# A joining stage whose first token tile is split: heads ahead of the line, weight rows taken in another order, gate rows loaded by another stage

## The chip, the cores and the metric

One NeuronCore of a Trainium2 chip runs the whole program in one launch. The metric is device microseconds (us) of that core, the median of several executions; lower is better. Engines: PE (TensorE, matrix products), DVE (VectorE), ACT (ScalarE), POOL (GpSimd), SP (SyncE, which here only issues DMAs and waits). Each engine runs its own instructions strictly in the written order, and the engines meet through semaphores.

## The reference, cut to what matters

The program is a two-layer transformer trunk (1024 image tokens and 256 context tokens, width 1024). The change is in the end of the first layer's mixer. Each token has a convolution branch of 512 channels and four attention heads of 128 channels; they are normed, joined and multiplied by one 1024 x 1024 weight:

```
def conv_module(a):
    u = a[..., :A_WIDTH] * jax.nn.sigmoid(a[..., A_WIDTH:])
    u = depthwise_conv(u, conv_w, conv_b)
    return jax.nn.silu(layer_norm(u, ln_g, ln_b))

def merge(ya, ob):
    yb = (rms_norm(ob, subln_g) * (1 - lambda_init)).transpose(0, 2, 1, 3).reshape(bsz, t, B_WIDTH)
    return jnp.concatenate([ya, yb], axis=-1) @ w_out
...
x = x + mx[2] * rms_norm(yx, norm_mix_post[i])
hx = modulate(rms_norm(x, norm_ffn_pre[i]), mx[3], mx[4])
```

## The kernel before, in words

The program is a chain of stages, each a block with one hand-written instruction list for each engine. A stage ends in a barrier that all five engines reach; then the semaphores are cleared, and a second barrier starts the next stage. The change is in the joining stage (`join_project`, signals and tiles named `out0_` or `out_`) and in the last lines of the stage ahead of it, the differential attention (`da_`), whose SP list already issues the joining stage's loads through the object `joined` (`JoinInputs`).

The joining stage works on ten tiles of 128 tokens, t = 0 to 9 (N = 10). A tile lies in `uo` as 8 blocks of 128 channels by 128 tokens: blocks 0 to 3 (AT = 4) are "the line" (the convolution branch, layer norm over its 512 channels), blocks 4 to 7 are the four heads (one rms norm each). For one tile:

- `mean(t)` on PE sums the line over channels with a matrix of ones; `centre(t)` on DVE takes the mean off the line.
- `square_heads(t)` and `square_line(t)` on ACT square both; `sums(t)` on PE adds the squares up over channels with one-column products (four for the heads, four for the line).
- `mean_squares(t)` on DVE, `inverse_roots(t)` on POOL (a power of -1/2 of 128x5 numbers) and `spread(t)` on PE (five transposes that put the factors along the tokens) give the norm factors; `normalise(t)` on DVE multiplies the line (L3299), then the heads (L3300).
- `finish(t)` on ACT takes four Silu of the line and rounds the whole tile to `y_hi`; `split(t)` on DVE takes the rest `y_lo`, and signals `y_ready`.
- The product on PE, `step(t, k, half)`, is three passes of 512 columns (hi*hi, hi*lo, lo*hi; L88 to L90) for each of 8 weight rows k and 2 halves of the output: 48 matmuls a tile.
- After it (`copy`, `residual`, `square_x`, `norm`, `turn`, `modulated`, `rest`) come the post norm with the gate rows, the residual with the old x, and the pre norm of the next stage.

LEAD = 2: while PE multiplies tile t, it also does `mean`, `sums` and `spread` of tile t + 2 between the products.

The weight rows have to be split too: `weights(k)` on ACT rounds row k of `work` to `w_hi` (signal `w_hi_done`), `weights(k)` on DVE takes the rest `w_lo` (signal `w_ready`). The eight raw rows lie in `work[:, 0..7]`, and the slots are used again: X = 2 means that the old x of tiles 0, 1, 2 goes to slots 2, 3, 4, so SP's `load_x(t)` waits until the row in that slot is split. Behind these loads SP's list has `inputs(2)`, the load of tile 2's tokens, which waits for `y_ready` of tile 0, because tile 2 takes tile 0's buffer; then the post gain into slot 7.

PE's list starts `mean(0)`, `sums(0)`, `mean(1)`, `spread(0)`, `sums(1)`, and then tile 0's product, which waits for `y_ready` of the whole tile and takes the rows in the order 0 to 7, with `spread(1)`, `mean(2)` and `sums(2)` between them; `spread(2)` follows the product. On ACT, `square_heads(t + 2)` stands ahead of `finish(t + 1)`; on DVE, `centre(t + 2)` stands ahead of `split(t + 1)`.

Of the kernel before, what the change touches and what calls it, by code (L numbers as in the profile page):

```python
# [15 lines left out]
P = 128  # L16
# [2541 lines left out]
def diff_attention(nc, head, joined, o_heads, qk, v_rows, ident, silu, mod, ada_w, ada_b, ada_first):  # L2558
# [60 lines left out]
    with ExitStack() as ctx:  # L2619
# [30 lines left out]
        def _(sp):  # L2650
# [321 lines left out]
def join_project(nc, joined, y_hi, y_lo, post_gain, x_old, x_new, ident, first, more_hi, more_lo, even_ps, sums_ps, first_acc,  # L2972
# [10 lines left out]
    POST, PRE = 0, 3  # L2983

# [3 lines left out]
    with ExitStack() as ctx:  # L2988
        def sb(label, shape, dt=F32):
# [11 lines left out]
        minus_half = sb("minus_half", [P, NORMS])  # L3001

# [10 lines left out]
            "x_done", "pre_squared", "pre_ms", "pre_rstd", "h_done", "h_turned", "f_done", "h_hi", "h_lo", "last_f", "last_hi"], inherited=joined.handles))  # L3013
# [14 lines left out]
        def _(sp):  # L3028
# [20 lines left out]
            for t in range(3):  # L3049
# [18 lines left out]
        def _(pe):  # L3068
# [12 lines left out]
            def sums(t):  # L3081
# [3 lines left out]
                if t == 1:  # L3085
                    pe.wait_ge(s.normed.sem, 1)
# [6 lines left out]
            def spread(t):  # L3093
# [3 lines left out]
                if t == 0:  # L3097
                    pe.wait_ge(s.centred.sem, 2)
                elif t == 1:
# [6 lines left out]
            def step(t, k, half):  # L3106
                cols_ = slice(half * BANK, (half + 1) * BANK)
                return exact_product(pe, ps[t % 2][:, cols_], y_hi[:, k, tokens(t)], y_lo[:, k, tokens(t)],
                                     w_hi.at(k)[:, cols_], w_lo.at(k)[:, cols_], k == 0, k == KD - 1)
# [13 lines left out]
            sums(0)  # L3123
            mean(1)
            spread(0)
            sums(1)
            for t in range(N + 2):
                if t >= 2:
# [19 lines left out]
                if t == 0:  # L3148
                    for k in range(KD):
                        pe.wait_ge(s.w_ready.sem, k + 1)  # L3150
                        for half in range(2):
                            mm = step(t, k, half)
                        if k == 0:
                            spread(1)
                        if k == 4:
                            mean(LEAD)
                        if k == 6:
                            sums(LEAD)
                    mm.then_inc(s.y_full.sem, 1)
                    spread(LEAD)  # L3160
                    continue
                for k in range(KD):
                    step(t, k, 0)
                    if k == 3:
                        mean(t + LEAD)
                for k in range(KD):
# [4 lines left out]
                spread(t + LEAD)  # L3171
# [1895 lines left out]
```

## Time and profile before

| | |
|---|---|
| median of 3 runs | 3247.48 us (3243.46 to 3247.98) |
| the profiled execution | 3244.99 us, of which the span of the profile is 3242.2 us |
| mean granted TensorE clock | 0.981 of full speed |
| PE busy | 3114.3 us, 96% of the span |
| DVE, ACT, POOL busy | 2196.7, 1358.1, 581.1 us |
| joining stage | from 615.7 us of the span to about 790 us |

Times below are us from the start of the span. "Idle before" an instruction is the time in which its engine did nothing ahead of it, with what ended that. A granted clock of 1.00 is the upper of TensorE's two levels (2.4 GHz), 0.50 the lower one (1.2 GHz).

### The profile page before, as it was taken

To read this page: it belongs to the slowest core of one execution; us is meant where nothing else is said; L and a number is where in the kernel's file an instruction comes from. 1 tells how busy PE (TensorE), PEld (TensorE's weight loads), DVE (VectorE), ACT (ScalarE), POOL (GpSimd) and SP (SyncE) were. 2 spreads that over 40 slices of the span, in tenths; PEclk is the share of its full clock that TensorE was granted. 3 is DMA by queue.
4 is the path that set the end of the run, shared out by engine and by line. 5 is a ranking of instruction groups with operands and counts; after the bars stand their busy time and mean duration, and the time that the engine had idled before them with its cause. 6 is when DMAs were issued, how large, how long until landed. Compare 5 with 4: busy or idle time off the path is not lost. (4 is left out here: it accounts for less than half of the span.)

```text
span 3242.2 us, 42850 instructions
## 1 busy us (share of the span) xinstructions
PE 3114.3 (96%) x16442; PEld 2557.2 (79%) x16442; DVE 2196.7 (68%) x2463; ACT 1358.1 (42%) x2275; POOL 581.1 (18%) x603
## 2 busy tenths in 40 slices
PE   7999899899999999999998999999999999999997
PEld 5888777788999999988797776666667788888875
DVE  4999767556756656679644346777774676776777
ACT  5222455466323323444565313444443433333444
POOL 0001000121222222233022100000001123332323
PEclk8999999899999999999999999999999999999998
DMA  7224786523122122566734743233312222222765
GB/s 219 69 93 133 220 264 219 195 98 90 57 73 79 56 78 69 181 212 201 240 129 148 260 145 70 46 84 71 73 36 78 85 83 80 85 78 89 241 205 196
DMA packets 302527, 415.70 MB, mean 128 GB/s; under 512 B 108878, under 2 KB 206862, under 8 KB 301302
## 3 DMA queue, kind: packets, MB, share of 16 engines
q1 hardware_dynamic: 288950, 363.29, 36.5%
q0 software_dynamic: 13376, 49.69, 4.1%
q8 instruction: 131, 2.15, 0.3%
q14 instruction: 70, 0.57, 0.1%
HBM read 318.65 MB, written 94.13 MB: 127 GB/s over the span
## 5 line engine op out<-in xcount | busy, mean ns | idle before, releaser
L2160 DVE TENSOR_TENSOR ring_lo<-raw_rows,ring_hi 128x512 fp32r<-128x512 f32 x200 | 181.8, 910 | 203.1 <-ACT ring_hi L2011 202.8
L4672 ACT ACTIVATE mla_e<-mla_scores 128x512 f32<-128x512 f32 x320 | 190.2, 598 | 307.9 <-PE mla_scores L90 297.0
L1283 PE MATMUL banks<-y_hi,ring_hi 128*128 128x384 f32 (+2 forms) x688 | 221.2, 322 | 4.5 <-DVEq L2148 3.9
L1285 PE MATMUL banks<-y_hi,ring_lo 128*128 128x384 f32 (+2 forms) x688 | 221.3, 322 | 0.0
L1284 PE MATMUL banks<-y_lo,ring_hi 128*128 128x384 f32 (+2 forms) x688 | 221.1, 321 | 0.0
L1283 PE MATMUL banks<-differences,ring_hi 128*128 128x512 f32 (+2 forms) x560 | 192.6, 344 | 3.4 <-ACT sums L2021 2.6
L1284 PE MATMUL banks<-differences,ring_hi 128*128 128x512 f32 (+2 forms) x560 | 192.3, 343 | 0.0
L1285 PE MATMUL banks<-differences,ring_lo 128*128 128x512 f32 (+2 forms) x560 | 192.2, 343 | 0.0
L862 DVE SCALAR_TENSOR_TENSOR ab_work<-ab_work,ab_taps 128x1295 f32<-128x1295 f32 x120 | 188.0, 1567 | 3.3
L4710 DVE TENSOR_REDUCE mla_least<-mla_rounded 128x1 f32<-128x1024 f32 x128 | 154.9, 1220 | 36.7 <-PE mla_rounded L4584 36.7
L2011 ACT ACTIVATE ring_hi<-raw_rows 128x512 fp32r<-128x512 f32 x200 | 125.2, 626 | 114.0 <-PE accs L1285 57.3
L1283 PE MATMUL accs<-y_hi,ring_hi 128*128 128x512 f32 (+1 forms) x464 | 165.9, 358 | 3.9 <-DVE ring_lo L3648 2.6
L1285 PE MATMUL accs<-y_hi,ring_lo 128*128 128x512 f32 (+1 forms) x464 | 165.6, 357 | 0.0
L1284 PE MATMUL accs<-y_lo,ring_hi 128*128 128x512 f32 (+1 forms) x464 | 165.5, 357 | 0.0
L2093 ACT ACTIVATE ring_hi<-raw_rows 128x512 fp32r<-128x512 f32 x154 | 97.1, 631 | 158.9 <-DMA raw_rows<-in_ffn_w_down 43.5
L4728 DVE TENSOR_TENSOR mla_acc<-mla_acc,mla_e 128x1024 f32<-128x1024 f32 x128 | 156.4, 1222 | 10.7 <-ACT mla_e L4672 5.1
L4616 PE MATMUL mla_out<-mla_e,ckv 128*64 128x512 f32 x640 | 155.0, 605 | 0.0
L2303 DVE TENSOR_TENSOR ring_lo<-raw_rows,ring_hi 128x512 fp32r<-128x512 f32 x154 | 125.3, 814 | 38.5 <-ACT ring_hi L2093 37.2
L1283 PEld LDWEIGHTS banks<-y_hi,ring_hi 128*128 128x128 f32 x688 | 129.7, 188 | 9.4 <-DVEq L2148 4.2
L1285 PEld LDWEIGHTS banks<-y_hi,ring_lo 128*128 128x128 f32 x688 | 129.8, 189 | 4.4
L1284 PEld LDWEIGHTS banks<-y_lo,ring_hi 128*128 128x128 f32 x688 | 129.8, 189 | 4.4
L88 PE MATMUL ab_main<-h_hi,da_first_k_hi 128*128 128x512 f32 (+1 forms) x360 | 131.4, 365 | 0.5 <-DVE da_first_k_lo L842 0.5
(561 smaller groups left out, 8711.2 us busy)
## 6 DMA issues: line engine op xcount, KB each, us to landing
raw_rows<-in_ffn_w_up SPq DMA_DIRECT2D x88, 512.0 KB, 3.6
da_ada_w<-in_ada_w SPq DMA_DIRECT2D x10, 4096.0 KB, 14.5
raw_rows<-in_ffn_w_down SPq DMA_DIRECT2D x110, 256.0 KB, 3.1
raw_rows<-in_ffn_w_down SPq DMA_DIRECT2D x44, 512.0 KB, 4.3
out_raw<-scratch_act SPq DMA_DIRECT2D x66, 256.0 KB, 3.4
sums<-scratch_act SPq DMA_DIRECT2D x55, 256.0 KB, 3.5
ab_raw<-in_ab_w_in SPq DMA_DIRECT2D x20, 512.0 KB, 3.9
scratch_act<-conv_lines SPq DMA_DIRECT2D x20, 512.0 KB, 4.8
```

The costliest lines, as they stand in the source:

```text
L88: pe.matmul(out, a_hi, b_hi, start=first, stop=False)
L862: dve.scalar_tensor_tensor(out=out, in0=src[:, j:j + SPAN], scalar=taps[:, i, j:j + 1], in1=out, op0=ALU.mult, op1=ALU.add)\
L1283: pe.matmul(out, w_hi[:, w], b_hi[:, a:a + n], start=start and k == 0, stop=False, skip_group_check=True)
L1284: pe.matmul(out, w_hi[:, w], b_lo[:, a:a + n], start=False, stop=False, skip_group_check=True)
L1285: mm = pe.matmul(out, w_lo[:, w], b_hi[:, a:a + n], start=False, stop=k == KD // 2 - 1, skip_group_check=True)
L2011: act.activation(blocks(begun.hi(r)), source(r), ACT.Copy).then_inc(s.w_hi, weight(r))
L2160: dve.tensor_tensor(blocks(begun.lo(r)), source(r), blocks(begun.hi(r)).bitcast(F32), ALU.subtract)\
L2303: dve.tensor_tensor(begun.lo(r), down_source(j, i), begun.hi(r).bitcast(F32), ALU.subtract).then_inc(s.down_lo, 1)
L4616: mm = pe.matmul(o_ps[c * C_V:(c + 1) * C_V, :], v[:, h % 2, kt, :], e[:, (h * KT + kt) % E_SLOTS, c * BANK:(c + 1) * BANK], start=kt == 0 ...
L4672: act.activation(e[:, tile % E_SLOTS, c * BANK:(c + 1) * BANK], s_ps[:, score_fill(h, i) % 3, :], ACT.Exp)\
L4710: dve.tensor_reduce(least[:, 0, t:t + 1], src, AX.X, ALU.max, negate=True).then_inc(s.piece_least.sem, 1)
L4728: dve.tensor_tensor(out, before, e[:, tile % E_SLOTS, :], ALU.add).then_inc(s.added.sem, 1)
```

## The change

Six column and gate loads (`load_rows`) leave the end of the attention stage's SP list and stand in the joining stage's SP list, behind its four stores and ahead of the x loads; their wait for stored modulation rows goes. Tile 0 is worked in two halves of channels. The heads have sums, mean square, inverse root, spread, norm, rounding and rest of their own, with signals of their own (`heads_...`), ahead of the line. The weight rows are rounded and split in the order `FIRST_ORDER` = 4, 5, 6, 7, 0, 1, 2, 3, and tile 0's product takes them in that order: four head rows once `heads_ready` is there, then four line rows once `y_ready` is there. What stood between PE's products is placed anew in tiles 0, 1 and 2. ACT touches a Silu of one column ahead of the first real one. The core of the diff:

```diff
             joined.load_tokens(sp, 0)
             joined.load_tokens(sp, 1)
-            sp.wait_ge(s.row0_stored.sem, 64)
-            sp.wait_ge(s.row1_stored.sem, 32)
-            joined.load_rows(sp)
...
                 if t < 3:
-                    sp.wait_ge(s.w_ready.sem, X + t + 1)
+                    sp.wait_ge(s.w_ready.sem, FIRST_ORDER.index(X + t) + 1)
...
             joined.store_tails(sp)
-            for t in range(3):
+            joined.load_rows(sp)
+            for t in (2, 0, 1):
                 load_x(t)
             sp.wait_ge(loaded.tail_stored.sem, 32)
             inputs(2)
...
+            def first_heads():
+                pe.wait_ge(s.squared.sem, 1)
+                for j in range(B_HEADS):
+                    mm = pe.matmul(head_ps[:, j:j + 1], sq[:, AT + j, :], ones[:, 0:1], start=True, stop=True)
+                mm.then_inc(s.heads_full.sem, 1)
...
+            def spread_first_line():
+                pe.wait_ge(s.rstd_done.sem, 1)
+                pe.wait_ge(s.centred.sem, 2)
+                pe.transpose(line_ps, rstd[:, 0, B_HEADS:NORMS].broadcast_to([P, P]), ident[:, :]).then_inc(s.spread.sem, 1)
...
             mean(0)
-            sums(0)
+            first_heads()
+            first_line()
+            spread_first_heads()
             mean(1)
-            spread(0)
-            sums(1)
...
+                if t == 0:
+                    pe.wait_ge(s.heads_ready.sem, 1)
+                    for n, k in enumerate(FIRST_ORDER):
+                        if k == 0:
+                            pe.wait_ge(s.y_ready.sem, 1)
+                        pe.wait_ge(s.w_ready.sem, n + 1)
+                        for half in range(2):
+                            mm = step(t, k, half, FIRST_ORDER)
+                        if k == AT:
+                            spread_first_line()
+                        if k == KD - 1:
+                            sums(1)
+                        if k == 1:
+                            spread(1)
+                    mm.then_inc(s.y_full.sem, 1)
+                    mean(2)
+                    continue
                 pe.wait_ge(s.y_ready.sem, t + 1)
...
                     step(t, k, 0)
+                    if t == 1 and k == 2:
+                        sums(2)
+                    if t == 1 and k == 6:
+                        spread(2)
...
                     mm = step(t, k, 1)
+                    if t == 1 and k == 1:
+                        mean(3)
-                    if k == 2:
+                    if k == (4 if t == 1 else 2):
                         sums(t + LEAD)
...
             act.wait_ge(loaded.small_in.sem, 48)
             square_heads(0)
-            weights(0)
-            weights(1)
+            for k in FIRST_ORDER[0:2]:
+                weights(k)
             square_line(0)
-            for k in range(2, 6):
+            for k in FIRST_ORDER[2:4]:
                 weights(k)
+            act.activation(table[:, :], gains[:, 0:1], ACT.Silu).then_inc(s.table.sem, 1)
+            round_first_heads()
+            weights(FIRST_ORDER[4])
             square_heads(1)
+            weights(FIRST_ORDER[5])
             square_line(1)
-            finish(0)
-            weights(6)
-            weights(7)
+            finish_first_line()
+            for k in FIRST_ORDER[6:]:
+                weights(k)
...
             mean_squares(1)
-            weights(6)
-            weights(7)
+            for n in range(6, KD):
+                weights(n)
             for t in range(N + 3):
                 normalise(t + 1)
+                if t == 1:
+                    residual(0)
                 centre(t + LEAD)
```

How the lists stand now is shown at three places. SP, at the end of the attention stage and the start of the joining stage (the two branches are the stage's end and the next one's start); before:

```order
L2927 DMA out_uo<-scratch_o_heads 128x4x128
L2944 DMA out_cols<-scratch_mod 128x8x1
L2946 DMA out_cols<-scratch_mod 128x8x1
L2944 DMA out_cols<-scratch_mod 128x8x1
L2946 DMA out_cols<-scratch_mod 128x8x1
L2949 DMA out_gates<-scratch_mod 128x1024 x2
L2619 UNCONDITIONAL_BRANCH
L3027 UNCONDITIONAL_BRANCH
L2918 DMA scratch_o_heads<-out_heads_out 128x256 x2
L2921 DMA scratch_mod<-out_mod_rows 4x256 x2
L3042 DMA out_work<-in_x 128x1024 x3
```

and now:

```order
L2924 DMA out_uo<-scratch_o_heads 128x4x128
L2619 UNCONDITIONAL_BRANCH
L3027 UNCONDITIONAL_BRANCH
L2915 DMA scratch_o_heads<-out_heads_out 128x256 x2
L2918 DMA scratch_mod<-out_mod_rows 4x256 x2
L2941 DMA out_cols<-scratch_mod 128x8x1
L2943 DMA out_cols<-scratch_mod 128x8x1
L2941 DMA out_cols<-scratch_mod 128x8x1
L2943 DMA out_cols<-scratch_mod 128x8x1
L2946 DMA out_gates<-scratch_mod 128x1024 x2
L3042 DMA out_work<-in_x 128x1024 x3
L2924 DMA out_uo<-scratch_conv 128x4x128
```

The six loads stand behind the branch to the next stage, and the three x loads still stand ahead of tile 2's tokens. PE, from the first mean of the joining stage to the first products (`out_sums` and `out_heads` are the banks of the sums, `accs` the output bank of tile 0, `ring` and `upper` the tiles that hold weight rows 4 to 7); before:

```order
L3078 MATMUL out_sums<-out_uo,out_ones 128x128 x4
L3088 MATMUL out_sums<-out_ones,out_sq 128x1 x4
L3090 MATMUL out_sums<-out_ones,out_sq 128x1 x4
L3078 MATMUL out_sums<-out_uo,out_ones 128x128 x4
L3101 MATMUL out_sums<-ident,out_rstd 128x128
L3103 MATMUL out_heads<-ident,out_rstd 128x128 x4
L3088 MATMUL out_sums<-out_ones,out_sq 128x1 x4
L3090 MATMUL out_sums<-out_ones,out_sq 128x1 x4
L88 MATMUL accs<-out_w_hi,y_hi 128x512
```

and now:

```order
L3079 MATMUL out_sums<-out_uo,out_ones 128x128 x4
L3108 MATMUL out_heads<-out_ones,out_sq 128x1 x4
L3114 MATMUL out_sums<-out_ones,out_sq 128x1 x4
L3120 MATMUL out_heads<-ident,out_rstd 128x128 x4
L3079 MATMUL out_sums<-out_uo,out_ones 128x128 x4
L88 MATMUL accs<-ring_hi,y_hi 128x512
```

`sums(1)` (L3088 and L3090 for the second time) is no longer ahead of the products; it follows the 24 matmuls of the head rows. DVE, from the first mean square of tile 0 to the last weight row (L3272 and now L3325 are `weights`, L3308 and now L3381 the rests `y_lo` of tile 0); before:

```order
L3290 TENSOR_SCALAR out_ms<-out_sums 128x4
L3291 TENSOR_SCALAR out_ms<-out_sums 128x1
L3272 TENSOR_TENSOR out_w_lo<-out_work,out_w_hi 128x1024
L3283 SCALAR_TENSOR_TENSOR out_uo<-out_sums,out_uo 128x512
L3272 TENSOR_TENSOR ring_lo<-out_work,ring_hi 128x1024
L3299 TENSOR_TENSOR out_uo<-out_uo,out_sums 128x512
L3300 SCALAR_TENSOR_TENSOR out_uo<-out_uo,out_gains,out_heads 128x512
L3272 TENSOR_TENSOR ring_lo<-out_work,ring_hi 128x1024
L3308 TENSOR_TENSOR y_lo<-out_uo,y_hi 128x8x128
L3290 TENSOR_SCALAR out_ms<-out_sums 128x4
L3291 TENSOR_SCALAR out_ms<-out_sums 128x1
L3272 TENSOR_TENSOR upper_lo<-out_work,upper_hi 128x1024 x2
```

and now:

```order
L3325 TENSOR_TENSOR upper_lo<-out_work,upper_hi 128x1024
L3370 SCALAR_TENSOR_TENSOR out_uo<-out_uo,out_gains,out_heads 128x512
L3325 TENSOR_TENSOR upper_lo<-out_work,upper_hi 128x1024
L3381 TENSOR_TENSOR y_lo<-out_uo,y_hi 128x4x128
L3336 SCALAR_TENSOR_TENSOR out_uo<-out_sums,out_uo 128x512
L3377 TENSOR_TENSOR out_uo<-out_uo,out_sums 128x512
L3325 TENSOR_TENSOR out_w_lo<-out_work,out_w_hi 128x1024 x2
L3381 TENSOR_TENSOR y_lo<-out_uo,y_hi 128x4x128
L3343 TENSOR_SCALAR out_ms<-out_sums 128x4
L3344 TENSOR_SCALAR out_ms<-out_sums 128x1
L3325 TENSOR_TENSOR out_w_lo<-out_work,out_w_hi 128x1024 x2
```

The last two weight rows are now rows 2 and 3 (whose slots take the x of tiles 0 and 1), and they still stand behind the mean square of tile 1 (now L3343).

## Rows read from the trace of the kernel before

**Rows 1.** Busy time by stretch; columns: stretch, length, engines' busy time, granted clock, DMA.

```profile
613.00:617.23 4.23, 1.19 (x9) 0.97 (x8) 0.60 (x3) 1.44 (x2) 0.10 (x1) 1.00 0.68 130
617.23:631.90 14.67, 10.46 (x46) 9.68 (x46) 11.04 (x16) 11.89 (x17) 2.04 (x1) 0.50 0.47 161
631.90:637.71 5.81, 5.81 (x16) 4.74 (x17) 3.69 (x6) 2.26 (x5) 2.08 (x1) 0.50 0.59 181
...
649.68:663.45 13.77, 13.77 (x76) 11.73 (x75) 7.53 (x10) 6.44 (x12) 3.11 (x5) 1.00 0.19 63
```

**Rows 2.** Timeline of PE; columns: start, duration, instruction, count, idle before.

```profile
618.89 1.86 PE L3088 MATMUL out_sums<-out_ones,out_sq 128*128 128x1 f32 x8 [1.70 <-ACT out_sq L3191]
...
626.03 1.06 PE L3103 MATMUL out_heads<-ident,out_rstd 128*128 128x128 f32 x4
...
631.90 0.80 PE L88 MATMUL accs<-out_w_hi,y_hi 128*128 128x512 f32 x1 [0.39 <-DVE y_lo L3308]
632.49 0.63 PE L89 MATMUL accs<-out_w_lo,y_hi 128*128 128x512 f32 x1
632.92 0.63 PE L90 MATMUL accs<-out_w_hi,y_lo 128*128 128x512 f32 x1
...
638.25 0.39 PE L89 MATMUL accs<-out_w_lo,y_hi 128*128 128x512 f32 x1
638.48 0.40 PE L90 MATMUL accs<-out_w_hi,y_lo 128*128 128x512 f32 x1
...
645.76 0.95 PE L3088 MATMUL out_sums<-out_ones,out_sq 128*128 128x1 f32 x8
...
649.16 0.32 PE L3101 MATMUL out_sums<-ident,out_rstd 128*128 128x128 f32 x1
...
649.68 0.48 PE L88 MATMUL out_ps<-out_w_hi,y_hi 128*128 128x512 f32 x1
```

**Rows 3.** Line L2619, the attention stage's end: instruction, duration in ns, start.

```profile
L2619 DVEq DRAIN  x1: 458/458/458, 613.1 to 613.1; - x1
L2619 SPq DRAIN  x1: 122/122/122, 614.6 to 614.6; - x1
```

**Rows 4.** Timeline of SP's DMA issues.

```profile
613.50 1.05 SPq L2949 DMA_DIRECT2D out_gates<-scratch_mod  x2
615.70 0.80 SPq L2918 DMA_DIRECT2D scratch_o_heads<-out_heads_out  x2
...
632.35 0.51 SPq L2927 DMA_DIRECT2D out_uo<-scratch_o_heads  x1
```

**Rows 5.** Timeline of POOL in the joining stage.

```profile
622.88 2.04 POOL L3411 TENSOR_TENSOR out_rstd<-out_ms,out_minus_half 128x5 f32<-128x5 f32 x1 [7.06 <-DVE out_ms L3291]
...
647.94 1.17 POOL L3411 TENSOR_TENSOR out_rstd<-out_ms,out_minus_half 128x5 f32<-128x5 f32 x1 [13.80 <-DVE out_ms L3291]
```

**Rows 6.** Timeline of DVE in the joining stage.

```profile
617.92 3.48 DVE L3272 TENSOR_TENSOR out_w_lo<-out_work,out_w_hi 128x1024 fp32r<-128x1024 f32 x3
...
627.12 0.69 DVE L3299 TENSOR_TENSOR out_uo<-out_uo,out_sums 128x512 f32<-128x512 f32 x1 [0.35 <-PE out_heads L3103]
...
630.62 1.23 DVE L3308 TENSOR_TENSOR y_lo<-out_uo,y_hi 128x1024 fp32r<-128x1024 f32 x1 [1.01 <-ACT y_hi L3202]
```

**Rows 7.** Timeline of ACT in the joining stage.

```profile
635.72 0.63 ACT L3185 ACTIVATE out_sq<-out_uo 128x512 f32<-128x512 f32 x1 [3.24 <-DMA out_uo<-scratch_o_heads]
636.65 1.65 ACT L3198 ACTIVATE out_uo<-out_uo,out_gains 128x128 f32<-128x128 f32 x4 [0.31 <-DVE out_uo L3299]
638.34 1.06 ACT L3202 ACTIVATE y_hi<-out_uo 128x1024 fp32r<-128x1024 f32 x1
```

**Rows 8.** Busy time by stretch, in the next stage.

```profile
845.90:849.30 3.40, 1.42 (x12) 1.22 (x11) 3.38 (x7) 3.40 (x7) 0.00 (x0) 1.00 0.00 0
849.40:852.70 3.30, 2.77 (x9) 2.80 (x10) 3.30 (x5) 1.43 (x3) 1.18 (x1) 0.50 0.00 0
```

**Rows 9.** Timeline of PE, in the next stage.

```profile
849.93 0.66 PE L1283 MATMUL banks<-differences,ring_hi 128*128 128x384 f32 x1 [2.61 <-ACT sums L2021]
```

More of the change, by code:

```diff
@@ L2983, in join_project @@
     POST, PRE = 0, 3
+    FIRST_ORDER = [*range(AT, KD), *range(AT)]
     def kind(t):
@@ L3147, in _ @@
                     pe.wait_ge(s.y_copied.sem, t - 1)
[L3148 to L3161, printed above, removed]
                 for k in range(KD):
                     step(t, k, 0)
-                    if k == 3:
+                    if t == 1 and k == 2:
+                        sums(2)
+                    if t == 1 and k == 6:
+                        spread(2)
+                    if t == 2 and k == 1:
+                        spread(3)
+                    if t > 1 and k == (5 if t == 2 else 3):
                         mean(t + LEAD)
+                if t == 2:
+                    turn(0)
                 for k in range(KD):
                     mm = step(t, k, 1)
-                    if k == 2:
+                    if t == 1 and k == 1:
+                        mean(3)
+                    if k == (4 if t == 1 else 2):
                         sums(t + LEAD)
                 mm.then_inc(s.y_full.sem, 1)
-                spread(t + LEAD)
+                if t > 1:
+                    spread(t + LEAD)
         @block.scalar
@@ L3191, in square_line, with round_first_heads, finish_first_line @@
                 act.activation(sq[:, 0:AT, :], uo[:, t % 2, 0:AT, :], ACT.Square).then_inc(s.squared.sem, 1)
+            def round_first_heads():
+                act.wait_ge(s.normed.sem, 1)
+                act.activation(y_hi[:, AT:KD, tokens(0)], uo[:, 0, AT:KD, :], ACT.Copy).then_inc(s.heads_hi.sem, 1)
+            def finish_first_line():
+                act.wait_ge(s.normed.sem, 2)
+                for k in range(AT):
+                    act.activation(uo[:, 0, k, :], uo[:, 0, k, :], ACT.Silu, scale=gains[:, k:k + 1],
+                                   bias=gains[:, AT + k:AT + k + 1]).then_inc(s.silu_done.sem, 1)
+                act.wait_ge(s.silu_done.sem, AT)
+                act.activation(y_hi[:, 0:AT, tokens(0)], uo[:, 0, 0:AT, :], ACT.Copy).then_inc(s.y_hi_done.sem, 1)
             def finish(t):
@@ L3302, in normalise, with first_heads_mean_squares, first_line_mean_square, normalise_first_heads @@
                                          op1=ALU.mult).then_inc(s.normed.sem, 1)
+            def first_heads_mean_squares():
+                dve.wait_ge(s.heads_full.sem, 1)
+                dve.tensor_scalar(ms[:, 0, 0:B_HEADS], head_ps[:, 0:B_HEADS], 1.0 / P, RMS_EPS, ALU.mult, ALU.add)\
+                   .then_inc(s.heads_ms.sem, 1)
+            def first_line_mean_square():
+                dve.wait_ge(s.stat_full.sem, 1)
+                dve.tensor_scalar(ms[:, 0, B_HEADS:NORMS], stat_ps[:, B_HEADS:NORMS], 1.0 / A_WIDTH, LN_EPS,
+                                  ALU.mult, ALU.add).then_inc(s.ms_done.sem, 1)
+            def normalise_first_heads():
+                dve.wait_ge(s.heads_spread.sem, 1)
+                heads = uo[:, 0, AT:KD, :]
+                dve.scalar_tensor_tensor(out=heads, in0=heads, scalar=gains[:, 2 * AT:],
+                                         in1=head_ps[:, :].rearrange("p (k n) -> p k n", n=P), op0=ALU.mult,
+                                         op1=ALU.mult).then_inc(s.normed.sem, 1)
+            def normalise_first_line():
+                dve.wait_ge(s.spread.sem, 1)
+                line = uo[:, 0, 0:AT, :]
+                dve.tensor_tensor(line, line, spread_over(line_ps), ALU.mult).then_inc(s.normed.sem, 1)
+            def split_first(done, ready, part):
+                dve.wait_ge(done.sem, 1)
+                dve.tensor_tensor(y_lo[:, part, tokens(0)], uo[:, 0, part, :], y_hi[:, part, tokens(0)].bitcast(F32),
+                                  ALU.subtract).then_inc(ready.sem, 1)
             def split(t):
```

51 lines of the change are left out of this document (35 added, 16 removed).

## The prediction, made before the changed kernel ran

> **What bounds the kernel now.** I read the page first (PE is busy 96% of the span), then the stretches of the joining stage, then PE's timeline with its idle times, and last what the other engines did where PE waited. Two things are to be seen. Ahead of the first product at 631.90 PE is starved: from 617.23 to 631.90 it is busy 10.46 of 14.67 us with small matmuls, and at the lower clock level (0.50), which stays until 637.71, 5.81 us after the first 512-column product [rows 1, 2]. From there on PE is the bound: in tile 1's stretch it is busy 13.77 of 13.77 us [rows 1]. So the change can gain only what lies ahead of 637.71 (idle PE, half clock), and every us of idle PE that it makes behind that point is paid back in full. By the end of tile 1's product both lists hold the same PE work (`mean` and `sums` of tiles 0 to 3, `spread` of 0 to 2, two products), so I compare there: before, tile 1 runs from 649.68 for 13.77 us, to 663.45 [rows 1, 2]. Behind it PE has the same work in both and nothing else limits it, so the difference stays.
>
> **Step 1, the barrier.** The attention stage ends with a drain on each engine. SP's starts at 614.6 and takes 0.12 us, behind the two gate loads at 613.50; DVE's, the next latest, starts at 613.1 and takes 0.46 [rows 3, 4]. Without the six loads the last arrival is 613.56 and not 614.72: the stage is released 1.2 us earlier, at 614.5 where it was 615.70 [rows 4]. The loads themselves now stand on SP's joining list. I cost them at nothing: behind them only x loads wait, and two of these wait until about 635 anyway (step 4). Their user `prepare` on DVE comes later still.
>
> **Step 2, the first product.** Before, it starts 16.2 us after the release (631.90 less 615.70). Now, in us after the release: mean, centring and square of the line stand where they stood, behind two weight rows, and PE can take the line's sums at 3.2 (618.89 less 615.70) [rows 2]. The heads' four one-column sums lie ahead of that, but take 1.86 at the lower level [rows 2] from 1.5, when the first mean is done: to 3.4. The line's sums: to 5.2. Beside them the heads' mean square on DVE (3.5) and POOL's power. The trace has no power of 128x4; of 128x5 it has 2.04 and 1.17 [rows 5]. The first ran beside DVE's weight rows, as this one will, so I take 2.04, to 5.6 (bounds 1.17 and 2.04). Four transposes, 1.06 [rows 2]: to 6.7. DVE norms four blocks, 0.7 as for the line's 0.69 [rows 6]: to 7.4. Then a weight row, 1.16 (3.48 for three), beside ACT's rounding of the half, and the rest `y_lo` of half a tile, 0.69 as a 512-column operation: to 9.3 [rows 6]. The first product comes at 614.5 + 9.3 = 623.8, 8.1 us earlier than before. ACT's early Silu only moves a table load, to where ACT waits for the normed heads. The matmul order of the weight rows costs nothing, since rounding and splitting follow the same order.
>
> On the power the Trainium skill has a rule ("SBUF — State Buffer", section "Who interferes with whom" and the reading of the diagram ahead of it): GpSimd and a VectorE instruction with two SBUF inputs take turns on a shared port pair, each for its whole instruction. The rows at 2.04 and 1.17 agree with it. By 1.17 the sum below would be 0.9 us shorter.
>
> **Step 3, tile 0.** I take the clock to come back 5.81 us after the first product, as before: at 629.6 (bounds: 2.8 us, the other return that I found, step 6, and not at all in tile 0, a rival). A pass is 0.43 us at the lower level (632.49 to 632.92) and 0.23 at the upper (638.25 to 638.48) [rows 2]. So 13 of the 24 passes on head rows, and the line's transpose, are done by 629.6; the other 11 take 2.5, to 632.1. Then `sums(1)`, twice 0.95 less its overlap, 1.7 [rows 2]: to 633.8. Line half and line weight rows are done meanwhile by ACT and DVE, which have little else. The four line rows (24 passes, 5.5) and `spread(1)` (0.52, 649.16 to 649.68 [rows 2]) end at 639.8. Before, that product ended some 9 us later, though with more of the small work done.
>
> **Step 4, the wait that takes the place of the old one.** DVE splits the last two weight rows behind the mean square of tile 1, so behind `sums(1)`: 633.8 + 0.25 + 2 x 1.16 = 636.4 [rows 6]. These are now rows 2 and 3, whose slots take the x of tiles 0 and 1. SP waits for them in order, and the tokens of tile 2 are queued behind: their second load is issued at about 637.3 (three issues of some 0.4). Before, it was issued at 632.35, and ACT had the tokens at 635.72, 3.37 us later [rows 4, 7]. Now two x loads of 512 KB run ahead of it: 640.7 at least, I take 641.1 (up to 641.7). Behind the tokens are queued, on ACT, `square_heads(2)` (0.63) and only then `finish(1)`, four Silu 1.65 and the rounding 1.06 [rows 7]; on DVE, `centre(2)` and only then `split(1)`, 1.23 [rows 6]. With overlaps that is 4.5 us: tile 1's product starts at 645.6. PE is done with tile 0 at 639.8 and has `mean(2)` alone (0.8) to do: 5.0 us idle. Before, the wait of ACT for these tokens (3.24 us [rows 7]) cost PE nothing, because PE was in the middle of tile 0.
>
> **Step 5, tile 1.** The 13.77 of before, and now also `sums(2)` (1.7) and `spread(2)` (0.5): 16.0. A second small wait: `residual(0)`, two 1024-column operations of some 1.2 each, now stands ahead of `centre(3)` on DVE, and `square_line(3)` and `sums(3)` follow. From `spread(2)` (7.0 into the tile) two norms 1.4, the post root some 0.8, residual 2.5, centre and square 1.25 make 12.9; PE is there at about 11.9. So 1.0, and the tile ends at 645.6 + 16.0 + 1.0 = 662.6, 0.85 earlier than 663.45.
>
> **Step 6, the clock in the new wait.** The clock fell after 613.00 to 617.23, where PE was busy 1.19 of 4.23 us, and again after 845.90 to 849.30, busy 1.42 of 3.40 [rows 1, 8]. Around the new wait PE is busy 0.8 of 5.8. I expect the clock to fall. After the second fall, products began at 849.93 behind 2.61 of idle time, and the upper level was back at 852.7, 2.8 us on [rows 8, 9]; after the first it took 5.81. Half of that time is lost: 1.4 to 2.9. I take 1.4, since there too a plain gap is followed by products alone. Sum: 662.6 + 1.4 = 664.0, 0.55 later than before.
>
> The Trainium skill says the same in general ("TensorE: Matmul & The Clock Gate", the table "Why this matters for your kernels"): a gap between bursts of matmuls drops the clock. It speaks against this change, and the rows agree. With it the sum is +0.55, without it -0.85.
>
> **Forecast.** No change that can be measured: 3244.99 (the profiled execution; its span is 3242.2) + 0.6 = 3245.6 us. The profiled execution lies 2.5 below the median of the runs shown and inside their range, so a median a little higher would not be against it. A measurement of this kernel can tell about 0.2% (6.5 us) from no change. Chance 0.50.
>
> **Rivals.**
> - *The clock holds in the wait*: 1.4 less, 3244.1. For it: `mean(2)` lies in the wait and breaks it. Against it: both falls shown came with PE busier than here. Chance 0.20.
> - *Tile 1 is not held up* (tokens and `y_lo` are there when PE comes): tile 1 at 640.6, end 657.6, 5.85 less: 3239.1. Against it: four links in a row (`sums(1)`, two weight rows, SP's order, ACT's order). Chance 0.12.
> - *Slower: the clock stays low through tile 0.* Then 11 head passes take 2.2 more and `sums(1)` 1.9 more, tile 1 starts at 649.7, at the lower level for 2.8 us more (1.4): end 668.1, 4.65 later, 3249.6. It decides against the change from a return 1.7 us later than in step 3 if the clock does not fall again, and at once if it does. For it: small matmuls kept the clock low for 14.67 us [rows 1], and `sums(1)` now stands amid the product. Against it: 24 passes run ahead of `sums(1)` with one transpose between. Chance 0.12.
> - *The barrier does not move*, another engine being as late as SP: 1.2 more, 3246.8. Against it: DVE's drain [rows 3]. Chance 0.06.
>
> **How the numbers follow.** The time is that of the forecast. The range 3239.5 to 3250.5 takes in the cases but for the outer part of the second and the third rival, and the unknown terms (power 0.9, landing 0.6, clock 1.5 either way). Faster by over 0.2% needs the second rival and all terms at their good end: 0.05. Slower by over 0.2% needs the third and a long return: 0.05. Within 0.2%: 0.90.
>
> **What would show it.** In the changed profile: the release near 614.5; the first product near 623.8, on `ring_hi`; the upper clock level from about 630; PE idle about 5 us ahead of tile 1, at about 640 to 646, with ACT waiting for the tokens of tile 2 ahead of `square_heads(2)`; a short wait ahead of `sums(3)`; tile 1 ending near 663 to 664, and no gap behind it. I am wrong if the wait ahead of tile 1 is under 2 us, or if a stage behind the joining stage changes by more than a us or two.

## The result, and the profile after

The changed kernel takes 3251.24 us (median of 20 runs, 3246.46 to 3259.49), the kernel before 3245.37 us beside it (20 runs, 3239.86 to 3251.29): ratio 1.0019, 95% interval 1.0012 to 1.0025, so some 6 us longer. I had forecast 3245.6 and a range up to 3250.5. The profiled execution took 3247.42 us (span 3245.5).

PE's timeline of the changed kernel, the rows behind idle time and others that the text below names (start, length, what was written and read, last the idle time ahead and what ended it):

```profile
614.98 1.16 PE L3079 MATMUL out_sums<-out_uo,out_ones 128*128 128x128 f32 x8 [1.84 <-DVE out_gains L3444]
615.97 0.95 PE L3108 MATMUL out_heads<-out_ones,out_sq 128*128 128x1 f32 x8
617.83 1.87 PE L3114 MATMUL out_sums<-out_ones,out_sq 128*128 128x1 f32 x8 [0.91 <-ACT out_sq L3227]
623.48 0.79 PE L88 MATMUL accs<-ring_hi,y_hi 128*128 128x512 f32 x1 [1.11 <-DVE y_lo L3381]
...
632.08 1.03 PE L3091 MATMUL out_sums<-out_ones,out_sq 128*128 128x1 f32 x8
...
638.91 0.39 PE L90 MATMUL accs<-out_w_hi,y_lo 128*128 128x512 f32 x1
642.43 2.07 PE L3079 MATMUL out_sums<-out_uo,out_ones 128*128 128x128 f32 x8 [3.13 <-DMA out_uo<-scratch_o_heads]
646.98 0.79 PE L88 MATMUL out_ps<-out_w_hi,y_hi 128*128 128x512 f32 x1 [2.48 <-DVE y_lo L3388]
...
662.46 1.05 PE L3089 MATMUL out_sums<-out_ones,out_sq 128*128 128x1 f32 x8 [0.78 <-ACT out_sq L3227]
...
667.16 0.63 PE L88 MATMUL accs<-out_w_hi,y_hi 128*128 128x512 f32 x1
...
684.52 0.48 PE L88 MATMUL out_ps<-out_w_hi,y_hi 128*128 128x512 f32 x1
```

The last two rows are the first products of tiles 2 and 3. The first product of tile 0 stands at 623.48 instead of 631.90 [rows 2]. Of these 8.4 us, 2.70 are left at tile 1's start (646.98 for 649.68): PE has waited 3.13 us for tile 2's tokens, and after `mean(2)` 2.48 us more for `y_lo` of tile 1. The stretches between the changes of the clock, the last one at the upper level cut once more ahead of `sums(3)` (start and end, length, then busy us and count of PE, PEld, DVE, ACT and POOL, the granted clock, DMA share, GB/s):

```profile
617.77:628.01 10.24, 9.06 (x31) 7.79 (x32) 7.26 (x10) 7.59 (x12) 2.83 (x2) 0.50 0.70 155
628.01:641.66 13.65, 11.29 (x60) 9.24 (x59) 6.13 (x9) 3.55 (x6) 2.09 (x1) 1.00 0.42 133
641.66:651.90 10.24, 7.00 (x22) 5.83 (x23) 1.92 (x2) 4.66 (x8) 0.00 (x0) 0.50 0.26 81
651.90:662.14 10.24, 9.78 (x55) 8.15 (x55) 7.87 (x14) 4.64 (x9) 1.92 (x3) 1.00 0.02 6
662.14:665.55 3.41, 3.09 (x22) 2.88 (x23) 1.62 (x4) 1.30 (x3) 1.55 (x3) 1.00 0.34 136
665.55:668.96 3.41, 3.41 (x10) 2.67 (x9) 0.00 (x0) 1.52 (x2) 0.82 (x1) 0.50 0.70 232
```

The clock is back 9.7 us earlier than before (628.01 for 637.71, [rows 1]), falls in the wait, and falls once more behind `sums(3)`, which I had not foreseen. How the tokens come late, in the timelines of SP, ACT and DVE:

```profile
614.64 0.81 SPq L2915 DMA_DIRECT2D scratch_o_heads<-out_heads_out  x2
...
620.30 15.69 SPq L3042 DMA_DIRECT2D out_work<-in_x  x3
636.10 0.38 SPq L2924 DMA_DIRECT2D out_uo<-scratch_conv  x1
636.52 0.51 SPq L2924 DMA_DIRECT2D out_uo<-scratch_o_heads  x1
...
642.41 0.63 ACT L3221 ACTIVATE out_sq<-out_uo 128x512 f32<-128x512 f32 x1 [10.82 <-DMA out_uo<-scratch_o_heads]
642.94 1.63 ACT L3246 ACTIVATE out_uo<-out_uo,out_gains 128x128 f32<-128x128 f32 x4
...
633.29 2.35 DVE L3325 TENSOR_TENSOR out_w_lo<-out_work,out_w_hi 128x1024 fp32r<-128x1024 f32 x2
...
645.69 1.23 DVE L3388 TENSOR_TENSOR y_lo<-out_uo,y_hi 128x1024 fp32r<-128x1024 f32 x1 [0.46 <-ACT y_hi L3250]
```

DVE splits the last weight rows until 635.64, SP holds its x loads until then, the tokens are issued behind them at 636.10 and 636.52, and ACT has them at 642.41, 5.89 us after the second issue. Before it was 3.37 [rows 4, 7]. Then come the square, the Silu, the rounding and `y_lo`.

**One count for all runs.** Executions differ by some 3 us ahead of the changed part already, so I count each tile's first product from the end of PE's last attention work (start of the first `mean` less its idle time: 614.98 less 1.84, 613.14, here). In the kernel before it is 616.03 less 3.00, 613.03; its row, and that of its first product of tile 3:

```profile
616.03 1.16 PE L3078 MATMUL out_sums<-out_uo,out_ones 128*128 128x128 f32 x8 [3.00 <-DVE out_gains L3364]
...
680.17 0.48 PE L88 MATMUL out_ps<-out_w_hi,y_hi 128*128 128x512 f32 x1
```

The table, one profiled execution for each row but for the ratios. Times in us; the last column but one is the start of tile 3 beside that of the kernel before:

| kernel | tile 0 | tile 1 | tile 2 | tile 3 | tile 3, beside before | ratio to before, 95% interval |
|---|---|---|---|---|---|---|
| before | 18.87 | 36.65 | 51.75 | 67.14 | | |
| changed | 10.34 | 33.84 | 54.02 | 71.38 | +4.24 | 1.0019, 1.0012 to 1.0025 |
| e1_tokens_first | 10.33 | 28.61 | 46.57 | 63.86 | -3.28 | 0.9989, 0.9978 to 1.0000 |
| e2_rows_only | 17.70 | 34.42 | 49.53 | 64.63 | -2.51 | 0.9990, 0.9979 to 1.0001 |
| e3_hold | 10.33 | 33.65 | 52.43 | 68.95 | +1.81 | 1.0008, 0.9996 to 1.0020 |
| e4_weights_first | 10.33 | 30.67 | 50.82 | 67.46 | +0.32 | 1.0007, 0.9997 to 1.0017 |
| e6_tokens_residual | 10.33 | 28.46 | 44.61 | 62.05 | -5.09 | 0.9991, 0.9983 to 1.0000 |
| e7_all | 10.33 | 27.83 | 44.00 | 61.85 | -5.29 | 0.9984, 0.9974 to 0.9993 |
| e9_residual_only | 10.34 | 32.92 | 54.74 | 72.42 | +5.28 | 1.0012, 1.0002 to 1.0022 |
| e10_hold_residual | 10.33 | 34.06 | 50.27 | 69.11 | +1.97 | 1.0011, 1.0002 to 1.0020 |
| e11_changed_again | 10.33 | 34.03 | 54.19 | 71.40 | +4.26 | 1.0011, 1.0002 to 1.0021 |
| e12_residual_again | 10.34 | 33.51 | 55.26 | 76.23 | +9.09 | 1.0016, 1.0006 to 1.0026 |
| e13_all_tokens | 10.33 | 27.63 | 43.80 | 60.26 | -6.88 | 0.9979, 0.9968 to 0.9989 |
| e14_hold_residual_tokens | 10.33 | 33.49 | 49.65 | 66.11 | -1.03 | 1.0002, 0.9992 to 1.0011 |

With 0.1% as 3.2 us, the stage's difference lies inside the measured interval in every run but e12 (there 9.1 for at most 8.4). So nothing behind this stage is needed to explain the times.

### The profile page after: what moved, and what is told of

Its sections match the earlier page's. It is cut to its first block and busy times, and to the rows that moved or that the text cites. A ratio compares the mean times of both kernels' runs of the same rounds, so it can differ in the third digit from the quotient of the medians.

```text
span 3245.5 us, 42853 instructions
## 1 busy us (share of the span) xinstructions
PE 3115.3 (96%) x16442; PEld 2556.4 (79%) x16442; DVE 2198.4 (68%) x2464; ACT 1359.4 (42%) x2277; POOL 581.3 (18%) x604
```

## The experiments

The theory after the result: the head start is spent in the wait for tile 2's tokens, in the clock that falls there, and in a second fall that a short wait ahead of `sums(3)` brings. Rivals: the move of the six loads costs something; the loss lies behind the stage; not SP's order but another link holds tile 1.

**e1, the tokens ahead of two x loads** (the changed kernel, SP's list):

```diff
-            for t in (2, 0, 1):
-                load_x(t)
+            load_x(2)
             sp.wait_ge(loaded.tail_stored.sem, 32)
             inputs(2)
+            for t in range(2):
+                load_x(t)
```

> The changed kernel with one edit in SP's list: tile 2's tokens are loaded ahead of the x of tiles 0 and 1. Theory (the head start is lost because the tokens are queued behind x loads that wait for the last weight rows): in the changed kernel's trace y_ready of tile 0 is there at 630.4, so the tokens are issued at about 631 and not 636.5, and land by about 635. Then tile 1 waits only for spread(1) (635.83), two norms, Silu, rounding and rest, and for mean(2) behind tile 0: it starts at about 642 and not 646.98, PE idle ahead of it about 2 us and not 5.6. Tile 1 ends 5 us earlier than in the changed kernel if the clock falls as it did, up to 8 if it holds: about 2 to 4 us earlier than the kernel before. Rival A (it is not SP's order; ACT or the landing itself holds tile 1): tile 1 starts at 646 to 647 as in the changed kernel, and the time stays there. Rival B (the loss is behind the joining stage): tile 1 is earlier, but the time stays about 6 us above the kernel before.

3244.05 us beside 3245.52. The timelines of SP, ACT and PE of this kernel:

```profile
633.58 0.51 SPq L2924 DMA_DIRECT2D out_uo<-scratch_o_heads  x1
636.85 1.48 SPq L3042 DMA_DIRECT2D out_work<-in_x  x2
...
637.12 0.63 ACT L3222 ACTIVATE out_sq<-out_uo 128x512 f32<-128x512 f32 x1 [2.87 <-DMA out_uo<-scratch_o_heads]
...
644.42 0.50 PE L88 MATMUL out_ps<-out_w_hi,y_hi 128*128 128x512 f32 x1 [1.91 <-DVE y_lo L3389]
657.62 1.05 PE L3090 MATMUL out_sums<-out_ones,out_sq 128*128 128x1 f32 x8 [0.72 <-ACT out_sq L3228]
```

Its stretches from the first return of the clock to the end of the second fall:

```profile
629.93:660.65 30.72, 28.09 (x159) 23.91 (x158) 18.19 (x29) 15.02 (x26) 5.50 (x7) 1.00 0.30 103
660.65:664.06 3.41, 3.41 (x9) 2.64 (x8) 0.00 (x0) 1.41 (x2) 0.88 (x1) 0.50 0.68 217
```

The tokens land 3.54 us after their issue, PE waits 1.91 us in place of 5.61, the clock holds through the wait, and the sign turns: 7.5 us less in the stage than in the changed kernel. That settles SP's order as the main cause. The short wait ahead of `sums(3)` and the fall behind it are still there.

**e2, the six loads alone moved** (the kernel before, `joined.load_rows(sp)` and its two waits taken from the attention stage, the call put behind `joined.store_tails(sp)`).

> The kernel before with one part of the change alone: the six column and gate loads stand in the joining stage. Theory: the barrier opens 1.2 us earlier, the first product starts at about 630.7 and not 631.90, and everything behind it is 1.2 us earlier; tile 1 ends at about 662.3 and not 663.45. Time 1.2 us below the kernel before, less than these rounds can tell. Rival (the loads cost more where they are now, since the x loads and the tokens of tile 2 are queued behind them): the x loads start later than 621.4, or the first product does not move.

3242.03 us beside 3245.52. The barrier's idle time falls from 3.00 to 1.83 us and the clock is back 17.07 us after its fall instead of 20.48. The first product comes 1.2 us earlier, as expected, and with the earlier return of the clock the stage gains 2.5 us where 1.2 was expected. The move gains in the stage, though the times alone do not tell it from no change; this rival is out.

**e3, dummy passes in the wait** (the changed kernel):

```diff
                     mm.then_inc(s.y_full.sem, 1)
+                    pe.wait_ge(s.normed.sem, 4)
+                    for _ in range(12):
+                        pe.matmul(head_ps[:, :], y_hi[:, 0, tokens(0)], w_hi.at(0)[:, 0:BANK], start=True, stop=True)
                     mean(2)
+                    for _ in range(14):
+                        pe.matmul(head_ps[:, :], y_hi[:, 0, tokens(0)], w_hi.at(0)[:, 0:BANK], start=True, stop=True)
```

> The changed kernel with 12 idle 512-column passes ahead of mean(2) and 14 behind it (written to the heads' bank, read by nobody), in the time in which PE waits for tile 1. Theory (a part of the loss is the clock that falls in that wait): tile 1 starts at about 647 as in the changed kernel, but at the upper level; the low stretch that began at 641.66 and ended at 651.90 is gone, tile 1 ends about 2.5 us earlier, at 664 to 665, and the time is about 2.5 us below the changed kernel's. Rival (the clock's fall costs nothing, because what follows waits for other engines): tile 1's passes are shorter, but a longer wait ahead of sums(3) takes the gain, and tile 1 ends within 0.5 us of 667.2.

3248.30 us beside 3245.52. The stretches of the wait and of the second fall in this kernel:

```profile
640.00:646.60 6.60, 6.15 (x30) 4.57 (x28) 1.90 (x2) 4.48 (x8) 0.00 (x0) 1.00 0.33 115
...
661.70:665.11 3.41, 3.41 (x10) 2.73 (x10) 0.89 (x3) 0.00 (x0) 1.73 (x2) 0.50 0.38 96
```

The low stretch in the wait is gone, tile 1 starts hardly earlier (33.65 for 33.84), and by tile 3 the stage is 2.4 us shorter than in the changed kernel: the price of that fall. Tile 2 starts only 1.6 us earlier (52.43 for 54.02, 2.5 expected), since the second fall stays and now lies wholly in tile 1.

**e4, the last two weight rows ahead of tile 1's mean square on DVE** (the changed kernel):

```diff
-            mean_squares(1)
             for n in range(6, KD):
                 weights(n)
+            mean_squares(1)
```

> The changed kernel with one edit in DVE's list: the last two weight rows are split ahead of the mean square of tile 1, in DVE's idle time from 630.4 to 633.15. Theory: the two x loads and behind them the tokens are released 2.6 us earlier (issue of the tokens at about 634 and not 636.5), POOL's power beside it takes nearer to 1.2 than 2.1 us, and tile 1 starts about 2.6 us earlier, at 644.4; the clock falls all the same. Time about 2.5 us below the changed kernel's, still above the kernel before. Rival (contention of the loads, not their release, sets the landing): the tokens land at 642 as before, because they then run beside other loads for longer, and tile 1 starts within 1 us of 646.98.

3247.68 us beside 3245.52. The tokens are issued at 635.45 and there at 640.8, 5.3 us later and still behind the x loads; PE waits 0.56 and 3.39 us. So the DVE link holds part of it, 3.2 us at tile 1's start, and the landing behind the x loads the rest. The clock falls all the same, but later and for less: it is low from 645.30 to 648.71, and by tile 3 the stage is 3.9 us shorter than in the changed kernel.

**e6, e1 and `residual(0)` behind `centre(3)` again**, as in the kernel before:

```diff
-                if t == 1:
-                    residual(0)
                 centre(t + LEAD)
...
-                if 2 <= t < N + 1:
+                if 1 <= t < N + 1:
                     residual(t - 1)
```

> Edit: the tokens of tile 2 ahead of the x loads of tiles 0 and 1 on SP, as before in this study, and residual(0) behind centre(3) again, as in the kernel before. The theory says that the wait of 0.7 us ahead of sums(3) and the clock's second fall (660.65 to 664.06 with the tokens edit alone) both come from residual(0) standing ahead of centre(3): then the wait goes, the clock holds through tile 1, and tile 2 starts 0.7 + 0.9 = 1.6 us earlier than with the tokens edit alone, tile 3 about 2.4 earlier; beside the kernel before, 5 to 6 us shorter (about 3240). Rival: the one-column sums themselves bring the clock down; then only the wait of 0.7 goes, the low stretch stays, and the time is 4 us shorter than before. Second rival: split(2) comes late behind residual(0) and a wait shows ahead of tile 2; then nothing is gained.

3243.30 us beside 3246.58. The wait ahead of `sums(3)` is gone and the clock holds to the end of the stage, with the same one-column sums in the same place:

```profile
629.51:677.73 48.22, 45.60 (x263) 39.07 (x261) 26.79 (x40) 27.07 (x49) 8.99 (x12) 1.00 0.36 116
```

So the sums alone do not bring the second fall; the wait ahead of them is needed for it. The stage gains 1.8 us on e1, less than the 2.4 expected, since 0.70 us of idle time stands ahead of `mean(4)`. The times of e1 and e6 do not differ measurably.

**e9, the same edit without the tokens'** (the changed kernel with `residual(0)` behind `centre(3)`).

> Edit: the changed kernel with residual(0) behind centre(3) again, and nothing else. By the theory the wait ahead of sums(3) (0.78 us) and the low stretch at 665.55 to 668.96 (1.7 us lost over tiles 1 and 2) go, and the long wait ahead of tile 1 with its fall stays: 2.5 us shorter than the changed kernel, so some 3 us longer than the kernel before where the changed one is 6 longer. Rival (the one-column sums bring the clock down by themselves): 0.8 us shorter than the changed kernel, with the low stretch still there behind sums(3).

3250.55 us beside 3246.58: not measurably shorter than the changed kernel. A miss: the wait ahead of `sums(3)` is gone, but the clock, fallen in the long wait, stays low to 658.95 where it was back at 651.90, so that 12.1 us of tile 1 run at the lower level and not 4.9: by halves some 3.6 us more lost. And PE now waits 0.94 us ahead of `mean(4)`.

**e7, four edits together**: e6, e4's order, and in tile 0's product `spread(1)` behind row 0 and `mean(2)` behind row 2.

> Edit: the tokens of tile 2 ahead of the x loads, residual(0) behind centre(3), the last two weight rows on DVE ahead of the mean square of tile 1, and in tile 0 spread(1) one weight row and mean(2) two weight rows earlier. By the theory all waits of PE in this stage are then under 1 us together: tile 1 starts about 1.4 us earlier than with the tokens edit alone, the clock does not fall again behind its return, and the kernel is 6 to 8 us shorter than before (3237.5 to 3239.5). Rival: mean(2) ahead of the last products of tile 0 waits for the tokens itself, with no work behind it to take its place; then the wait ahead of tile 1 stays at about 2 us and the time is that of the run with the tokens and residual edits.

3242.31 us beside 3246.58: shorter than both kernels. PE waits 0.52 us ahead of tile 1, which starts 0.8 us earlier than in e1 (1.4 expected), and the clock does not fall again in the stage. But 1.13 us stand ahead of `mean(4)`, so the waits together were not under 1 us.

**e10, e3 and e9 together**: clock held, residual behind the centring.

> Edit: the changed kernel with 26 dummy 512-column passes in the wait ahead of tile 1, which hold the clock up there, and with residual(0) behind centre(3). Both low stretches behind the first return of the clock should be gone, and the wait for tile 2's tokens stays, now filled with passes that compute nothing. By the theory what is left is the forecast without its term for the clock and with the landing as measured: tile 1 starts 1.4 us later than I predicted and the product runs on at the upper level, -0.85 + 1.4 = +0.5 us beside the kernel before: no change, ratio 0.9995 to 1.0007, 5 us shorter than the changed kernel. Rival (the time is lost elsewhere, not in the clock): it stays 4 to 6 us longer than the kernel before.

3249.30 us beside 3246.90. The clock holds through all of it, but the stage is 2.0 us longer than before, where 0.5 was expected. DVE, SP and PE of this kernel show what was left out:

```profile
660.29 1.22 DVE L3393 TENSOR_TENSOR y_lo<-out_uo,y_hi 128x1024 fp32r<-128x1024 f32 x1
...
662.51 0.75 DVE L3422 TENSOR_SCALAR out_work<-out_work,out_small 128x1024 f32<-128x1024 f32 x1 [0.86 <-POOL out_small L3506]
...
660.40 0.33 SPq L3046 DMA_DIRECT2D scratch_x<-out_work  x1
664.52 0.35 SPq L3042 DMA_DIRECT2D out_work<-in_x  x1
664.91 0.43 SPq L2924 DMA_DIRECT2D out_uo<-scratch_conv  x1
665.38 0.51 SPq L2924 DMA_DIRECT2D out_uo<-scratch_o_heads  x1
...
669.90 1.16 PE L3079 MATMUL out_sums<-out_uo,out_ones 128*128 128x128 f32 x8 [2.11 <-DMA out_uo<-scratch_o_heads]
```

Tile 4's buffer is free at 661.51, but its tokens are queued behind the x load of tile 3, which is issued 4 us after the store of the x in its slot. That load waits for two things: for the norm of tile 0 (L3422), which ends at 663.26, and for the store to land, which is the later one here. In e7 and e9 the norm is the later one (it ends at 659.66 in e7, and the load is issued at 659.74). `residual(0)` behind `centre(3)` makes the store later (13.6 us after tile 1's first product, 11.9 in e3): the wait of 0.7 us ahead of `sums(3)` is traded for one ahead of `mean(4)`, and e10 gains nothing on e3. In e9 the same wait, 0.94 us, is the smaller part of the loss; the longer low stretch is the greater.

**e11 and e12, the changed kernel and e9 once more.**

> The changed kernel itself, a second profile and times beside the two others of this call. Open: whether the low stretch around the wait ahead of tile 1 (10.24 us in its first profile, 17.07 us in that of the kernel with residual(0) behind centre(3)) is of that length in each execution. If it varies from one execution to another, this profile shows another length, and the times of the two kernels overlap; if the length belongs to the kernel, it is 10.24 again with a second fall behind sums(3). Time about 6 us longer than the kernel before.

> The changed kernel with residual(0) behind centre(3), a second profile and times beside the changed kernel of this call. If the long low stretch (17.07 us) belongs to it, it is there again and the kernel gains nothing over the changed one beyond its wait of 0.8 us; if it was that one execution, the low stretch is shorter here, no second fall follows, and the times come out 2 to 3 us shorter than those of the changed kernel.

3252.47 and 3253.29 us beside 3246.90. The low stretch around the wait in the first profile of the edit (e9):

```profile
641.88:658.95 17.07, 14.18 (x44) 11.96 (x45) 4.94 (x10) 6.13 (x11) 1.36 (x2) 0.50 0.15 49
```

In its second one (e12):

```profile
644.12:661.19 17.07, 14.06 (x44) 11.93 (x45) 4.93 (x10) 6.01 (x11) 1.28 (x2) 0.50 0.16 50
```

And in the second profile of the changed kernel (e11), with its second fall:

```profile
642.50:652.74 10.24, 6.70 (x21) 5.54 (x21) 1.92 (x2) 4.66 (x8) 0.00 (x0) 0.50 0.27 87
666.39:669.80 3.41, 3.41 (x10) 2.65 (x9) 0.00 (x0) 1.25 (x2) 0.96 (x1) 0.50 0.69 219
```

Each kernel shows its own length of the low stretch in both of its profiles, so in two profiles each a variation of it from one execution to another is not borne out. The changed kernel's row of the table is repeated (+4.24, +4.26). That of the edit is not (+5.28, +9.09): in e12 PE waits 2.80 us ahead of `mean(4)` where it was 0.94 in e9, and the clock falls once more there. Why the return differs between the two kernels is open: up to it PE's list is the same in both.

**e13 and e14, the tokens ahead of the x load in SP's loop too**, on e7 and on e10:

```diff
+            inputs(3)
             for t in range(1, N + 1):
-                inputs(t + 2)
...
                 store_x(t - 1)
+                inputs(t + 3)
                 load_x(t + 2)
```

> Edit: the kernel with all four edits (tokens first, residual(0) behind centre(3), weight rows first, spread and mean earlier), and SP's loop now issues the tokens of tile t + 3 ahead of the x load of tile t + 2, which waits until the x stored ahead of it has landed. In the kernel without this last edit, PE waits 1.13 us ahead of mean(4), until the tokens of tile 4 are there, issued at 660.12 and 660.60; the rest y_lo that frees their buffer ends at 657.91. By the theory the tokens are issued at 657.9 and 658.3, landed 4.5 us later at 662.8, ahead of mean(4) at 664.2: the wait goes, tile 3 starts 1.1 us earlier, and the kernel is 5 to 7 us shorter than before. Rival: the x load that is issued later makes a wait of its own further on, or the tokens land as late as before since other transfers hold them; then the time stays where it was without this edit.

> Edit: the kernel with dummy passes in the wait ahead of tile 1 and residual(0) behind centre(3), and the same new order in SP's loop. That kernel came out 2.4 us longer than the one before where 0.5 was expected, and its profile has a wait of 2.11 us ahead of mean(4), for tile 4's tokens, which were issued 3 us behind the end of y_lo. If that wait is what was missing in the expectation, it goes here and the kernel is level with the one before (0 to +1 us). Rival: the missing time is elsewhere, and the kernel stays 2 to 3 us longer than before though the wait is gone.

3238.47 and 3246.34 us beside 3245.78. The timelines of SP and PE of e13:

```profile
656.63 0.36 SPq L2924 DMA_DIRECT2D out_uo<-scratch_conv  x1
657.03 0.57 SPq L2924 DMA_DIRECT2D out_uo<-scratch_o_heads  x1
658.44 0.34 SPq L3042 DMA_DIRECT2D out_work<-in_x  x1
...
641.87 0.50 PE L88 MATMUL out_ps<-out_w_hi,y_hi 128*128 128x512 f32 x1 [0.52 <-DVE y_lo L3391]
```

Its stretch from the return of the clock to the start of tile 3:

```profile
628.14:674.50 46.36, 45.56 (x261) 38.88 (x261) 26.71 (x40) 27.27 (x49) 8.09 (x12) 1.00 0.38 125
```

The same stretch of e14:

```profile
627.99:680.48 52.49, 51.67 (x288) 43.87 (x287) 27.08 (x40) 26.82 (x49) 8.99 (x12) 1.00 0.35 111
```

The wait ahead of `mean(4)` is gone in both, and PE is busy but for 0.8 us of its stretch. e14 is level with the kernel before, as expected, though PE still computes nothing of use in the long wait. So the wait for tile 4's tokens is what was missing in the expectation for e10. e13 is 7 us shorter than the kernel before, the best kernel here.

## Why the prediction was wrong

The mechanism was right as far as it went; two of its terms, the landing of tile 2's tokens and the clock's loss in the new wait, were sized too small, and a third, a second fall of the clock, was put at nothing. On the count of the table I forecast tile 1's end 0.55 us later than before. It came 3.60 later (54.02 less 50.42), and 4.24 by tile 3.

1. *The barrier* was right: release at 614.64 for 614.5.
2. *The first product* was right, 623.48 for 623.8, by a somewhat shorter path: the heads' sums ran at the upper level (0.95 us at 615.97, where I took 1.86), the clock falling only at 617.77, and POOL's power took 1.88, not 2.04, and ended at 619.15. So the line's sums, and not the power, came last ahead of the heads' transposes. That the power is short without a weight row beside it is borne out less than I wrote: the row at 1.17 [rows 5] had multiplications of the gate rows beside it on DVE from 648.36.
3. *Tile 0* was right and slightly pessimistic: clock back at 628.01 for 629.6, 4.5 us after the first product; `sums(1)` done at 633.1 for 633.8.
4. *The new wait* came where I said and for the reason given. The term that failed is the landing: 5.89 us where I took 3.8 (at most 4.4), on no row of a load behind two others. I had priced the two x loads ahead as a small addition to [rows 4, 7]. With the tokens first it is 3.54 (e1), 3.31 (e7). Since step 3 ended earlier, tile 1 came 1.4 us later than forecast (646.98 for 645.6).
5. *Tile 1* was right: 0.78 us of wait where I took 1.0, and the 16.0 of work.
6. *The clock* was mis-sized. It fell as forecast, but was low for 4.92 us of tile 1, a loss of 2.46; I took the shorter of the two returns I had, 1.4, with 2.9 as the bound. That is 1.06 too little. And I priced the wait ahead of `sums(3)` as its own length and put a fall of the clock behind it at nothing, without a reason: the clock was low for 1.61 us of tile 1 and 1.80 of tile 2, so 0.8 and 0.9 lost.

The sum: 0.55 + 1.3 (tile 1's start, less the 0.11 by which the attention stage ended later) + 1.06 + 0.8 - 0.1 (the other parts of step 5) = 3.6. e3 gives 2.4 for the first fall; e14, without a fall, ends tile 1 0.77 us earlier than before (49.65 for 50.42), near the -0.85 that I had without the clock's term; there the start of tile 1, 0.9 us later than forecast, and the missing wait ahead of `sums(3)` balance. The rival *clock holds* fell at once, *tile 1 not held up* is what e1, e6, e7 and e13 made of it (-3.3 to -6.9), *the clock stays low through tile 0* did not come, and *the barrier does not move* fell too (614.64 for 615.70). The ratio of 1.0019 still lies within the 0.2% to which I gave 0.90, but only just, and 20 runs tell it from no change. The 4.2 us of the stage alone would make 3249.2, inside the range; the median lies 0.7 above its end. No run shows a cost for the rest, and the interval (3.9 to 8.1 us longer) takes in the 4.2. But the landing and both falls of the clock went the same way, and my bounds did not add them.

On the clock the Trainium skill ("TensorE: Matmul & The Clock Gate", section "Why this matters for your kernels") says that idle gaps between bursts of matmuls take the speed away. The long wait and e3 agree (0.50 from 641.66, and 2.4 us back with the gap filled). In e1 the clock held through a gap of 1.91 us. The second fall came behind a gap of only 0.78 us.

## What to carry to other kernels

When a stage's start is made faster, ask what the next item needs and what stands ahead of it in each queue: here one order on SP turned 4.2 us lost in the stage into 3.3 gained, and with the other edits into 6.9. In a list that is issued strictly in order, as SP's is, a load that someone waits for goes ahead of loads that themselves wait. Price a wait of PE together with the clock that it may cost, and a move that removes one wait together with the wait that it makes one tile later.

## What the runs showed of the hardware that was not expected

- A load of tokens took 5.2 to 6.2 us from its issue to its first use behind two 512 KB loads just issued (changed kernel 5.89, e9 5.20, e10 6.17), and 3.3 to 3.5 us ahead of them (e1, e7), all issued by SP. Whether their place in the order or the traffic beside them makes the difference was not separated.
- The clock fell behind 0.7 to 0.8 us of idle time that was followed by one-column sums (changed kernel, e1, e3, e4, e11), in the changed kernel with PE busy for 12.87 of the 13.65 us between its return and this fall. It held in e7 and e10 through idle times of 1.13 and 2.11 us that were followed by 128-column sums, and fell in e12 in one of 2.80 us followed by the same sums.
- With one PE list up to that point, it came back 4.9 and 4.6 us after tile 1's start in the changed kernel's profiles and 12.1 and 12.0 us after it in those of e9 and e12, with PE busy all the while in e9 (12.11 of 12.11 us). The cause is open.
